# Chosen rows of an expert layer made by one-hot products on TensorE in place of a store and an indirect gather

## The reference

```
aff = softmax(h @ w_router)                       # 512 x 16
top_aff, top_idx = lax.top_k(swapaxes(aff, 1, 2), cap)
xe  = h[top_idx]                                  # chosen rows: 16 x 64 x 1024
hid = silu(xe @ w_gate[e]) * (xe @ w_up[e])       # 16 x 64 x 1024
ye  = hid @ w_down[e] * top_aff
y   = zeros(L, D).at[top_idx].add(ye)             # back to the tokens
x   = x + g2 * y;  return rmsnorm(x, norm_f)
```

## Time and profile before

| what | value |
|---|---|
| median of 3 runs | 2975.1 us |
| profiled execution, its own time | 2975.89 us |
| its span | 2974.1 us |
| PE busy | 2849.5 us (96%), 17316 instructions |
| DVE, ACT, POOL busy | 1623.3, 1014.0, 261.3 us |
| mean granted TensorE clock | 0.985 of full speed |
| moved | 444.61 MB, mean 149 GB/s |

### The profile page before, as it was taken

How to read it: one execution, slowest core, us unless ns; L and a number is a source line. 1 busy time by engine, 2 the same in 40 slices (tenths; PEclk the granted TensorE clock), 3 DMA queues, 4 the chain that set the end, 5 groups by cost and what they waited for, 6 DMA issues and landing times.

```text
span 2974.1 us, 41823 instructions
## 1 busy us (share of the span) xinstructions
PE 2849.5 (96%) x17316; PEld 2218.9 (75%) x17316; DVE 1623.3 (55%) x3044; ACT 1014.0 (34%) x2084; POOL 261.3 (9%) x288
## 2 busy tenths in 40 slices
PE   8999999999999999999999999999999997998887
PEld 6888877888888888888887888888788886343333
DVE  6876686465655565454575565454555764221112
ACT  4222363563332343232353552222334452000002
POOL 0000012230000000000022330000000730000000
PEclk9999999999999999999999999999999998999999
DMA  5454421122232222222221113222322018999998
GB/s 203 180 211 162 181 98 57 44 72 99 93 117 89 99 86 93 86 78 89 83 84 43 58 65 106 88 96 92 110 70 77 13 77 327 412 424 426 424 425 341
DMA packets 59870, 444.61 MB, mean 149 GB/s; under 512 B 6816, under 2 KB 7072, under 8 KB 22688
## 3 DMA queue, kind: packets, MB, share of 16 engines
q1 hardware_dynamic: 56544, 430.12, 37.7%
q0 software_dynamic: 1696, 6.55, 0.6%
q10 hardware_dynamic: 1440, 5.25, 0.5%
HBM read 436.40 MB, written 5.51 MB: 149 GB/s over the span
## 4 chain that ended last, share of the span: by engine, by line
PE 78%; DMA 10%; DVE 8%; ACT 3%; issue 1%; POOL 1%; ACTq 0%; SPq 0%; DVEq 0%; POOLq 0%
PE ps L234 77%; DMA b<-in_eg 6%; DVE b L244 3%; DVE b L254 2%; DMA b<-in_ed 2%; PE ps L368 1%; DVE b L780 1%; ACT b L260 1%; DMA b<-in_wu 1%; ACT b L470 1%; POOL b L244 1%; DVE b L2316 0%; DMA b<-in_wd 0%; ACT b L259 0%; DVE b L249 0%
## 5 line engine op out<-in xcount | busy, mean ns | idle before, releaser
L234 PE MATMUL ps<-b,b 128*128 128x512 f32 (+9 forms) x14138 | 2660.4, 375 | 79.9 <-DVE b L254 19.8
L234 PEld LDWEIGHTS ps<-b,b 128*128 128x128 f32 (+4 forms) x14138 | 2041.5, 177 | 652.5 <-issue 194.5
L244 DVE TENSOR_TENSOR b<-b,b 128x512 f32<-128x512 f32 (+8 forms) x752 | 625.6, 838 | 296.4 <-ACT b L470 216.4
L470 ACT CAST b<-b 128x1024 fp32r<-128x1024 f32 (+2 forms) x408 | 392.1, 963 | 413.9 <-PE ps L234 323.8
L244 DVE TENSOR_TENSOR b<-ps,b 128x64 f32<-128x64 f32 (+6 forms) x437 | 174.9, 420 | 278.2 <-PE ps L234 188.1
L244 POOL TENSOR_TENSOR b<-b,b 128x1024 fp32r<-128x1024 f32 (+8 forms) x163 | 185.9, 1160 | 1215.1 <-ACT b L2393 505.6
L260 ACT ACTIVATE b<-b 128x512 f32<-128x512 f32 (+7 forms) x304 | 155.7, 521 | 233.7 <-DVE b L254 172.3
L254 DVE SCALAR_TENSOR_TENSOR b<-ps,b,b 128x128 f32<-128x128 f32 (+4 forms) x225 | 110.8, 540 | 170.7 <-PE ps L234 95.1
L244 DVE TENSOR_TENSOR b<-b,ps 128x512 f32<-128x512 f32 (+2 forms) x118 | 77.1, 660 | 221.2 <-PE ps L234 219.0
L234 PE MATMUL ps<-b 64*64 64x64 f32 (+10 forms) x2704 | 174.9, 262 | 20.5 <-DVE b L244 10.7
L254 DVE SCALAR_TENSOR_TENSOR b<-b,b 128x512 f32<-128x512 f32 (+6 forms) x296 | 176.4, 610 | 27.3 <-ACT b L260 23.7
(11 more groups left out here) (121 smaller groups left out, 614.9 us busy)
## 6 DMA issues: line engine op xcount, KB each, us to landing
b<-in_eu SPq DMA_DIRECT2D x28, 2048.0 KB, 34.7
b<-in_wg SPq DMA_DIRECT2D x44, 1024.0 KB, 4.8
b<-in_wu SPq DMA_DIRECT2D x44, 1024.0 KB, 4.8
b<-in_win SPq DMA_DIRECT2D x40, 1024.0 KB, 4.8
b<-in_ed SPq DMA_DIRECT2D x19, 2048.0 KB, 33.3
b<-in_wd SPq DMA_DIRECT2D x48, 768.0 KB, 4.2
b<-in_eg SPq DMA_DIRECT2D x29, 1024.0 KB, 27.4
b<-in_eg SPq DMA_DIRECT2D x14, 2048.0 KB, 33.1
```

The source lines that it names most:

```text
L234: return e.h.matmul(out, l, r, start=start, stop=stop)
L244: return e.h.tensor_tensor(out, a, b, op)
L470: e.h.copy(hi, src).then_inc(*self.S.tick(("hi", i)))
```

## The change

The store, the gathers, their counters and the index `ixT` are gone. The chosen rows are made by TensorE instead: the one-hot rows `oh` of a pair (128 chosen x 512 tokens) are transposed in four 128x128 pieces into PSUM bank 0 (`oht_pe`), ACT copies them to `self.oht`, which lies in the first half of `xe` (`oht_act`), and `xT_pe` multiplies the kept rows `self.ht` with them: for each of eight pieces of 128 columns four float32 products that add up over the tokens, straight into the turned form that the transposes gave before. `oh_dve` is cut out of `xT_dve` and runs earlier, behind `hid(pr, 0)` of the pair before. `self.ht` now stays until pair 7's rows are made, so its two places leave the ring: 20 places, of which 14 are filled in turn.

```
-            [a] for a in (*k.ring.slots, k.b4f, worn, *half(k.hTf), yef, later_a, *half(htf), later_b, k.early)]
+            [a] for a in (*k.ring.slots, k.b4f, worn, *half(k.hTf), yef, later_a, later_b, k.early)]
...
-        self.ring = Once(k, "e_landed", self.slots, (6, 7, 16, 17, 20, 21),
-                         ((0, 1), (2, 3), (4, 5), (8, 9), (10, 11), (12, 13), (14, 15), (18, 19)))
+        self.oht = v3(self.xe[:, 0:512], 4)
+        self.ring = Once(k, "e_landed", self.slots, (6, 7, 16, 17, 18, 19),
+                         ((0, 1), (2, 3), (4, 5), (8, 9), (10, 11), (12, 13), (14, 15)))
...
-        before[6] = before[20] = [(self.P, ("ht", 7))]
-        before[18] = before[19] = [(self.gat[0], 0)]
-        for n in (21, 0, 1, 2, 3, 4, 5, 12, 13, 16, 8, 9, 10, 11, 14, 15, 17, 7):
-            self.load_first(e, n)
-        for i in range(4):
-            e.wait_ge(S.at(("ht", 2 * i + 1)))
-            e.h.dma_start(k.hd.ap()[i * 128:i * 128 + 128, :], self.ht[:, i, :]).then_inc(*self.dma["h"].tick(i, 16))
-        for n in (20, 6, 18, 19):
+        before[6] = before[18] = [(self.P, ("ht", 7))]
+        for n in (19, 0, 1, 2, 3, 4, 5, 12, 13, 16, 8, 9, 10, 11, 14, 15, 17, 7, 18, 6):
             self.load_first(e, n)
...
+    def oht_pe(self, e, pr):
+
+        e.wait_ge(self.V.at(("oh", pr)), self.V.at(("hid", pr - 1, 0)) if pr else self.S.at(("ht", 3)))
+        for t in range(4):
+            p = self.k.tr(e, self.k.bank[0][:, t * 128:t * 128 + 128], self.k.two[pr % 2][:, t * 128:t * 128 + 128])
+        p.then_inc(*self.P.tick(("oht", pr)))
+
     def xT_pe(self, e, pr, h):
 
-        e.wait_ge(self.gat[pr].at(0))
         if pr:
             e.wait_ge((self.S if h else self.V).at(("hidT", pr - 1, h)))
-        self.tr_pe(e, "xT", pr, h, self.xe)
+        e.wait_ge(self.S.at(("oht", pr)), self.S.at(("ht", 7)))
+        for c in range(4):
+            f = slice(512 * h + 128 * c, 512 * h + 128 * c + 128)
+            for t in range(4):
+                p = mm(e, self.k.bank[6 + h][:, c * 128:c * 128 + 128], self.ht[:, t, f], self.oht[:, t, :], t == 0, t == 3)
+        p.then_inc(*self.P.tick(("xT", pr, h)))
...
+        self.oht_pe(e, 0)
         for h in range(2):
             self.xT_pe(e, 0, h)
...
                 if m == 2:
                     self.hidT_pe(e, pr, 0)
+                    if pr < 7:
+                        self.oht_pe(e, pr + 1)
...
+    def oht_act(self, e, pr):
+        e.wait_ge(self.P.at(("oht", pr)))
+        e.h.copy(self.oht, v3(self.k.bank[0][:, :], 4)).then_inc(*self.S.tick(("oht", pr)))
...
-        e.wait_ge(self.dma["h"].at(3), V.at("ixT"))
-        for pr in range(8):
-            if pr:
-                e.wait_ge(P.at(("xT", pr - 1, 1)))
-            e.h.indirect_dma_start(self.xe, None, k.hd.ap(),
-                                   bass.IndirectOffsetOnAxis(ap=self.ixT[:, pr:pr + 1], axis=0)).then_inc(
-                *self.gat[pr].tick(0, 16))
-        e.wait_ge(P.at(("w", 7, 3, 0)), self.S.at(("row", 2)))
+        e.wait_ge(P.at(("xT", 7, 1)), self.S.at(("row", 2)))
```

More of the change, by code:

```diff
@@ L3442, in __init__ @@
         inner = span(m.O, SLOT)
+        inner = span(m.O, SLOT)
         self.slots = [[a] for a in (*half(k.low), m.utf, m.rawf[:, 0:SLOT])] + [
             [tables, states[:, 512:1024]], [k.rowsf[:, 0:SLOT]], [inner], [span(k.sw, 1024), k.rstd, states[:, 0:512]]] + [
-            [a] for a in (*k.ring.slots, k.b4f, worn, *half(k.hTf), yef, later_a, *half(htf), later_b, k.early)]
+            [a] for a in (*k.ring.slots, k.b4f, worn, *half(k.hTf), yef, later_a, later_b, k.early)]
         self.idx, self.ixT = k.memu[:, 0:64], k.memu[:, 64:72]
-        self.dma = {n: k.count(f"d_{n}") for n in ("h",)}
-        self.gat = [k.count(f"gather{i}") for i in range(8)]
-        self.ring = Once(k, "e_landed", self.slots, (6, 7, 16, 17, 20, 21),
-                         ((0, 1), (2, 3), (4, 5), (8, 9), (10, 11), (12, 13), (14, 15), (18, 19)))
-        assert sorted(self.ring.wide) == [0, 2, 8, 10, 14, 18]
+        self.oht = v3(self.xe[:, 0:512], 4)
+        self.ring = Once(k, "e_landed", self.slots, (6, 7, 16, 17, 18, 19),
+                         ((0, 1), (2, 3), (4, 5), (8, 9), (10, 11), (12, 13), (14, 15)))
+        assert sorted(self.ring.wide) == [0, 2, 8, 10, 14]
         self.stored = [k.count(f"out_x{i}") for i in range(5)]
@@ L3692, in act @@
                 *S.tick(("ht", m)))
+        self.oht_act(e, 0)
         for pr in range(8):
@@ L3695, in act @@
             for h in range(2):
+                if h and pr < 7:
+                    self.oht_act(e, pr + 1)
                 e.wait_ge(P.at(("w", pr, 2 * h, 1)))
@@ L3787, in final_dve @@
         for i in range(4):
-            e.wait_ge(S.at(("root", i // 2)), S.at(("row", 3)), P.at(("w", 7, 3, 0)))
+            e.wait_ge(S.at(("root", i // 2)), S.at(("row", 3)), P.at(("xT", 7, 1)))
             stt(e, self.out[:, i, 512:1024], self.xt[i][:, 512:1024], self.ms[:, 12 + i:13 + i], self.rows[3], ALU.mult,
@@ L3798, in final_x, with oh_dve @@
         tt(e, x, x, self.zbank(j, i), ALU.add).then_inc(*self.V.tick(("x", j, i)))
-    def xT_dve(self, e, pr):
+    def oh_dve(self, e, pr):
         P, V = self.P, self.V
@@ L3804, in xT_dve @@
         ts(e, self.oh[pr % 2], self.iot, self.ixf[:, pr:pr + 1], ALU.is_equal).then_inc(*V.tick(("oh", pr)))
+    def xT_dve(self, e, pr):
+        P, V = self.P, self.V
         for h in range(2):
@@ L3869, in dve @@
         e.wait_ge(V.at("step"))
-        tt(e, self.ixT, self.ixf, self.far[:, 8:16], ALU.add).then_inc(*V.tick("ixT"))
         tt(e, self.ixf, self.ixf, self.far[:, 8:16], ALU.add).then_inc(*V.tick("ixf"))
+        e.wait_ge(V.at("ixf"), self.G.at("iota"))
+        self.oh_dve(e, 0)
         e.wait_ge(V.at("best"))
         ts(e, self.vT, self.best, 0.5, ALU.mult).then_inc(*V.tick("vT"))
-        e.wait_ge(V.at("ixf"), self.G.at("iota"))
         self.xT_dve(e, 0)
@@ L3885, in dve @@
                 tt(e, self.hid[:, h * 512:h * 512 + 512], t, B[2 * h + 1][:, :], ALU.mult).then_inc(*V.tick(("hid", pr, h)))
+                if h == 0 and pr < 7:
+                    self.oh_dve(e, pr + 1)
                 if h == 0:
```

## The result

Four runs of the changed kernel have a median of 2985.4 us (2981.8 to 2990.0), against 2974.9 us (2974.3 to 2975.2) for the kernel before. The ratio is 1.0038, 95% interval 1.0023 to 1.0053: **slower**, by more than the 0.2% that the prediction took as the least that can be told from no change. Predicted were 2984.5 us and 2974 to 2991.

What follows compares the result with a forecast made beforehand. PE sets the pace in the stage's first half, DMA in the second. PE's side 9.5 us later and transfers 10.2 us later gave 9.4 us on the median of 2975.1: 2984.5 us, range 2974 to 2991.

Steps and rivals of the forecast that it cites:

- The start: From one-hot rows to first weight products in the expert layer: 4.0 us later, bounds 2.6 and 5.7 us.
- The price of a product: One float32 product of 128 columns on PE: 0.245 us at full clock, 0.49 us at half clock.
- The dry stretch: Weight queue in the first pass: empty for 11 us until PE frees piece 20's place, where before 1 to 3.
- The transfers' end: Last weight transfers of the expert layer: end at 2965.7 against 2955.5, 10.2 us later.
- Two sides within a microsecond: End of the expert layer: PE 9.5 us later and transfers 10.2 us later, so 9.4 us taken.
- PE's side: PE's work to the layer's end, never waiting for transfers: passes of 55.6 us, ending at 2972.5, 9.5 us later.
- the transfers' side: Weight queue with 20 places: late first refill, dry stretch, then 158 pieces, ending 10.2 us later.
- PE's idle time behind 2655: PE's idle time after 2655 us in the profile: falls from 29.4 us to under 6.
- the late first refill: Weight queue at the layer's start: first refill's data flows from 2528.9, where before the queue flowed from 2519.0.
- the places: Ring of weights: 20 places, 14 refilled; those refills last 34.6 us and the fifteenth waits for piece 20's place.
- The fed queue: Rival: transfers alone decide and the queue never runs dry, 1.7 us faster, 2973.4 us; chance 0.16.
- Dear products: Rival: unhidden weight loads make a PE product dearer than 0.245 us, up to 0.376 us and 3018 us; chance 0.08.

Runs made afterwards that it cites:

- after: First profile of the changed kernel: span 2980.0 us, of which 492.7 us from POOL's iota to the end.
- again: The changed kernel profiled once more, nothing altered: span 2986.6 us, of which 491.3 us from POOL's iota to the end.
- before: First profile of the kernel before the change: span 2974.1 us, of which 482.4 us from POOL's iota to the end.
- before_again: The kernel before the change profiled once more, on another chip: span 2968.4 us, of which 484.0 us from POOL's iota to the end.
- double: Changed kernel with every product of the chosen rows made twice: 542.9 us from POOL's iota to the end, span 3033.5 us.
- bytes: Changed kernel plus 14 unread loads of 256 KB that give back the gathers' bytes: 499.6 us from POOL's iota to the end, ratio 1.0052.
- quarter: Changed kernel with one product in place of four per piece of the chosen rows: 481.9 us from iota to end, ratio 0.9991 to the kernel before.
- split: Changed kernel with the fifteenth refill issued as two 1 MB loads instead of one of 2 MB: 492.2 us from iota to end, ratio 1.0035.

## Why the prediction was right

**The start.** Predicted were 4.0 us more, by a start worth full clock, with bounds of 2.6 and 5.7. From the one-hot rows to the first weight product it was 13.4 us in after, where the prediction had 13.6 (from 2511.3 to 2524.9). The clock rose inside the products (mean 0.55 in the window from 2510 to 2515, 1.00 in the next), near the middle that was taken. In `again` it was 12.1 us. The other side of the difference varies too: the start of the kernel before, made worth full clock in the same way, is 9.5 us in `before` and 11.3 in `before_again`. The first pair gives the 4.0 us; the means give 2.4. So the start was over-sized, and the agreement of the first pair was partly luck.

**The price of a product.** 0.245 us was taken. Passes tell it best: 62.15 - 55.0 = 7.15 us for 32 products and their gaps in `double` is 0.223 us; a pass of 55.0 us in place of the predicted 55.6 says 0.23. It was over-sized by 6 to 10%. The Trainium skill's four passes (FP8 and Floating Point Precision, section TensorE Precision Notes) gave 0.213 us as an estimate; the measured price lies between that and the one taken. As the prediction said, the end hardly hangs on it.

**The dry stretch.** Predicted: 11 us, since 14 refills last to 2564 and the fifteenth waits for piece 20. It came in the place named and for the reason named, some 9 us long. Counted from the first weight product, the refills ran out at 39.8 us (39.1 forecast) and the load that ends the gap went out at 47.5 (48.0 forecast); the rest is that data flowed within a microsecond of that issue, where 2.5 us had been taken.

**The transfers' end.** Predicted 10.2 us later. From the iota, the transfers end at 463.0 and 463.9 us in the two profiles of the kernel before and at 472.2 and 471.1 in the two of the changed kernel: 9.2 us later in the first pair, 8.2 by the means.

**Two sides within a microsecond.** This step did not come out. The prediction had PE's side, if it never waits, end 9.5 us later, and the transfers' side 10.2. With passes of 55.0 us PE's side was over-sized by some 4 us, and with it the forecast of two equal limits. PE waited 6.2 us for transfers in after, and `double` gives the same margin: of 57 us more work 6 were covered. So PE's side lies some 6 us under the end that the layer had, and it was the transfers' side that set it: `bytes` lengthened the transfers by 7.7 us and the stage followed by 7.6, while `quarter` took 5.4 us a pass from PE and gained only what the refills gained. `split` cannot tell the two limits apart, since it hardly moved the transfers. The sum was right because the side that decides was sized within 1 to 2 us. PE's idle time behind 2655 was 5.2 us, where under 6 was forecast.

**The balance.** By experiments that change one thing: two places 6.2 us, three quarters of the products 10.1 us, the gathers' bytes -7.6 us, sum 8.7. Measured between the means of two profiles each: 8.8 us. That the two agree to 0.1 us is luck: a stage varies by 1.5 us, the fourth quarter of the products and the new transposes are in no term, and two of the terms meet in the same dry stretch. The prediction's 9.4 us was right in size and in its main steps, the late first refill, the places and the dry stretch.

**The rivals.** The fed queue, with the rule behind it that the engine with the highest use is the one to relieve (the Trainium skill, Trace Analysis, section Identifying the Most-Contended Engine): the queue stood empty for 9 us, so it did not come about. `bytes` shows that its price was right, only that it was paid back elsewhere. Dear products: they did not come about either, at 0.223 to 0.231 us a product.

**What the prediction did not see** is the spread ahead of the layer. Three runs of before within 0.4 us looked like a quiet kernel; 30 runs spread over 15 us. The median of four runs agreed with 2984.5 partly by luck of the draw.

## What to carry to other kernels

Where weights stream through a ring of places, draw up a ledger: when does the queue run dry, and which step of the consumer frees the next place? Until the transfers have caught up with the consumer, a place is worth about one piece of transfer time, and every microsecond of the consumer's work ahead of the place that the queue waits for is worth about a microsecond. Later in the stage such work could be taken away here without gain (`quarter`), and added only up to the 6 us that PE still waited (`double`). Fewer bytes counted nearly in full (`bytes`), but the queue stood empty for want of room, and what was saved was paid back twice: 6.2 us for the places, 10.1 for the products.

## What the runs showed of the hardware

- The same instructions ahead of the layer took 2483.7 to 2497.0 us in twelve profiles, with 18 to 51 us of PE's work at half clock in them, and the more of it, the later. A comparison of a few microseconds in 3000 needs a clock that starts with the stage in question, or some ten runs of each kernel.
- A start at half clock is not a fixed price. The clock rose 3.3 and 6.1 us behind the first of the 32 products in two executions of the same kernel, and 14.0 us behind it when the products were half as long: that took 2.6 us from the start (28.9 us from the iota to the first weight product, against 31.5), and 3 us came back in the weight products behind.
- A load that goes out earlier is worth only what it brings the loads behind it: the one of `split` went out 1.8 us sooner and moved the transfers' end by 0.5 us, because the next one still waited for its place.
